# Three weight loads of 2 MB moved on SyncE's DMA queue, between two layers of a one-core kernel

## What is computed

```python
p = h @ w_in                                   # 1024 -> 3 x 1024
p = sum(pp[:, j:j + L] * conv_w[j] for j in range(3)) + conv_b
x0, x1, v = split(p, 3)
h_fwd, h_bwd = hyena_filter(L, w1, b1, w2, b2, w3, freq)
z = v * x1
z = bidir_long_conv(z, h_fwd, h_bwd) + bias * z
y = (x0 * z) @ w_out
```

## Time and profile before

| | |
|---|---|
| Time, median of 3 runs | 1439.36 us (1438.39 to 1439.51) |
| The profiled execution's own time | 1443.63 us, span 1441.70 us |
| Mean granted TensorE clock | 0.968 |
| TensorE busy | 1300.4 us (90%) |
| VectorE busy | 641.2 us (44%) |
| ScalarE busy | 300.6 us (21%) |
| HBM read | 496.57 MB, 348 GB/s over the span |

### The profile page before, as it was taken

The page is one execution under the profiler, slowest core; times in us unless marked ns, Lnnn a source line. Parts: engine busy times, 40 slices in busy tenths (PEclk is TensorE's granted clock), DMA queues, the critical chain, the costliest instruction groups (busy, mean ns, idle before and its releaser), DMA issues.

```text
span 1441.7 us, 21888 instructions
## 1 busy us (share of the span) xinstructions
PE 1300.4 (90%) x9044; PEld 676.9 (47%) x9044; DVE 641.2 (44%) x1175; ACT 300.6 (21%) x508; POOL 60.2 (4%) x112
## 2 busy tenths in 40 slices
PE   4999888899999979889898999999999978988898
PEld 1445335764444424333345776874454433333344
DVE  5998862254333322222333678854433322232232
ACT  2226341321111111111112113131111111111111
POOL 0010581000000000000000000000000000000000
PEclk9999999999999999999998999989999999999999
DMA  9663874959999999999999872587999999999996
GB/s 380 226 212 87 162 221 183 394 233 376 417 421 421 426 427 427 429 423 430 426 418 341 316 275 117 217 351 298 372 425 422 422 428 426 425 430 428 428 420 271
DMA packets 54327, 502.78 MB, mean 349 GB/s; under 512 B 9740, under 2 KB 16652, under 8 KB 20236
## 3 DMA queue, kind: packets, MB, share of 16 engines
q1 hardware_dynamic: 53676, 499.18, 86.3%
q10 hardware_dynamic: 544, 2.10, 0.4%
HBM read 496.57 MB, written 4.69 MB: 348 GB/s over the span
## 4 chain that ended last, share of the span: by engine, by line
PE 61%; DMA 28%; DVE 7%; issue 2%; SPq 1%; ACT 1%; DVEq 0%; ACTq 0%
PE ps L753 56%; DMA arena<-in_w_experts 23%; DMA arena<-in_ada_w 4%; PE ps L1071 2%; PE ps L446 2%; SPq L490 1%; DVE arena L2052 1%; ACT arena L1419 1%; DVE arena L1879 0%; DMA arena<-in_mcst 0%; DVE arena L2245 0%; PE ps L806 0%; DVE arena L1874 0%; DVE arena L1875 0%; DVE arena L1892 0%
## 5 line engine op out<-in xcount | busy, mean ns | idle before, releaser
L753 PE MATMUL ps<-arena 128*32 128x512 f32 (+10 forms) x8224 | 1216.1, 485 | 122.2 <-issue 44.9
L753 PEld LDWEIGHTS ps<-arena 128*32 128x32 f32 (+5 forms) x8224 | 614.7, 130 | 708.4 <-issue 582.2
L1419 ACT ACTIVATE arena<-ps 128x512 f32<-128x512 f32 (+6 forms) x305 | 168.5, 552 | 923.3 <-PE ps L753 767.5
L1419 ACT ACTIVATE arena<-arena 128x256 f32<-128x256 f32 (+7 forms) x143 | 94.6, 683 | 152.6 <-DVE arena L2113 58.3
L2093 DVE SCALAR_TENSOR_TENSOR arena<-arena,ps 128x256 f32<-128x256 f32 x44 | 21.2, 481 | 228.4 <-ACT arena L1419 228.4
L2111 DVE CAST arena<-ps 128x512 bf16<-128x512 f32 x42 | 29.1, 692 | 165.5 <-PE ps L753 165.5
L2048 DVE COPY arena<-ps 128x512 f32<-128x512 f32 x44 | 30.4, 692 | 128.4 <-PE ps L753 128.4
L2081 DVE TENSOR_TENSOR arena<-arena 128x1024 bf16<-128x1024 f32 x42 | 51.5, 1226 | 37.3 <-ACT arena L1419 37.0
L1071 PE MATMUL ps<-arena 128*128 128x128 f32 x352 | 52.8, 273 | 0.0
L2113 DVE TENSOR_TENSOR arena<-ps,arena 128x1024 f32<-128x1024 f32 x42 | 51.4, 1225 | 1.4
L743 POOL MEMSET arena<- 128x1 f32 x2 | 0.2, 102 | 1186.2 <-PE ps L1071 1186.2
(11 more groups left out here) (234 smaller groups left out, 483.6 us busy)
## 6 DMA issues: line engine op xcount, KB each, us to landing
arena<-in_w_experts SPq DMA_DIRECT2D x70, 3072.0 KB, 20.6
arena<-in_w_experts SPq DMA_DIRECT2D x98, 1024.0 KB, 13.6
arena<-in_w_experts SPq DMA_DIRECT2D x38, 2048.0 KB, 19.7
arena<-in_ada_w SPq DMA_DIRECT2D x40, 1024.0 KB, 6.7
arena<-in_hy_w_in SPq DMA_DIRECT2D x6, 2048.0 KB, 13.7
arena<-in_ada_w SPq DMA_DIRECT2D x4, 2048.0 KB, 23.0
arena<-in_w_shared SPq DMA_DIRECT2D x2, 3072.0 KB, 10.1
arena<-in_hy_w_out SPq DMA_DIRECT2D x1, 4096.0 KB, 12.1
```

Of the source, the lines that this page charges most:

```text
L753: return pe.matmul(out, lhsT, rhs, start=start, stop=stop, skip_group_check=skip)
L1419: return act.activation(out, in_, func, **kw)
```

## The change

The loads of the first three parts of the Hyena input matrix leave `moe_loads(0)`, where they stood between the waits for `dn_mm` (NG - 1) and `dn_mm` (DOWNS). Part 0 is now issued behind `moe_loads(0)`, which ends with the check for crowded experts, and ahead of the wait for `moe_x`; part 1 behind `f_w2` and ahead of block 16; part 2 behind the last of `fw_in` and ahead of block 17. Nothing else is changed.

```diff
                 if li == 0:
                     sp.wait_ge(sem("hscr_out"), 16)
                     sp.wait_ge(sem("dn_mm"), NG - 1)
-                    for n in range(3):
-                        load(hyw[:, n], A["hy_w_in"][HYP[n]], f"hyw_in{n}")
                 sp.wait_ge(sem("dn_mm"), (li + 1) * DOWNS)
                 sp.wait_ge(sem("hscr_out"), 16 * (li + 1))
...
             first_experts(0, (2,))
             moe_loads(0)
 
+            load(hyw[:, 0], A["hy_w_in"][HYP[0]], "hyw_in0")
             sp.wait_ge(sem("moe_x"), KD)
...
             load(at(HC["zemb"], L), A["hcst"][:, HCST["zemb"][0]:HCST["zemb"][0] + L], "fw_in")
             load(f_w1, A["f_w1"], "fw_in")
             load(f_w2, A["f_w2"], "fw_in")
+            load(hyw[:, 1], A["hy_w_in"][HYP[1]], "hyw_in1")
             ada_load(LATER)
             load(f_w3, A["f_w3"], "fw_in")
             for name in ("ic", "is"):
                 load(at(HC[name], L), A["hcst"][:, HCST[name][0]:HCST[name][0] + L], "fw_in")
             for name, width in (("decay", HYW), ("fc", P), ("fs", P)):
                 load_by_parity(HC[name], name, width)
+            load(hyw[:, 2], A["hy_w_in"][HYP[2]], "hyw_in2")
             for n in range(3, 6):
                 ada_load(LATER + 2 * n - 5)
```

## The result

| | before | changed | ratio, 95% interval |
|---|---|---|---|
| median of 6 runs | 1437.93 us | 1451.44 us | 1.0091 [1.0076, 1.0106] |
| the changed kernel once more, beside 23 runs of before | 1439.61 us | 1448.41 us | 1.0062 [1.0043, 1.0080] |
| profiled execution, span | 1441.7 us | 1447.9 us | |

Slower, by 13.5 us in the first comparison and 8.8 us in the second. The two profiled executions differ by 6.2 us only, and that has a reason which all later readings must respect: the stretch ahead of the change, the same instructions in both kernels, ended 4.0 us sooner in the changed kernel's profile.

A forecast was written before the change was run, and what follows sets the result against it. Between the layers the bound was taken to be block 17's second half, landing behind a DMA backlog. Its delay of 6.9 us plus 1.8 us of low clock gave 1439.4 + 8.7 = 1448.1 us; range 1445.5 to 1450.5, 8 in 10 1442.5 to 1452.0.

The forecast's parts named there:

- the two terms of the sum: Between MoE layer 0 and project(1): block 17 landing later, +6.9 us, and TensorE's lowered clock behind that wait, +1.8 us.
- Step 1: SyncE's dn_mm waits lose their loads: SyncE gains nothing and the expert loads are not sped up.
- Step 2: SyncE's exit from the crowded-expert branch: taken as 0.5 us, hyw 0 issued at 769.5 and landing at 776.4, ahead of project(0).
- Rival C: SyncE leaves the check's branch as slowly as TensorE, delaying hyw 0 and everything behind it: 1453.4 us, chance 0.10.
- Step 3: Crowded-expert check of layer 0: gets cheaper without hyw loads on the DMA engines, 3.4 us taken, between zero and 3.8.
- Step 4: SyncE's queue behind the check: hyw 1 issued at 775.0, block 17 landing at 808.2 against 801.3, +6.9 us.
- Step 5: Block 17's second half is asked for at 789.9, before the queue runs dry, full until 808: no cost.
- Step 6: TensorE's wait for block 17 lowers its clock: 3.5 us at half rate behind it, +1.8 us, bounds 0 and 2.6.
- Step 7: From 802.38 to the filtered spectrum TensorE sets the chain, with no wait group above 1.0 us up to 946: the shift stays.
- The sum: Whole kernel: 6.9 us for block 17 plus 1.8 us for the clock, 8.7 us slower, 1448.1 us.
- Rival A: Cheaper check is kept and block 17 isn't late, as hyw loads fill the small-packet stretch: -3.4 us, 1436.0 us, chance 0.11.
- Rival B: Most idle queue time is filled in the small-packet stretch: block 17 at 803.8, +2.5, no clock drop, 1441.9 us, chance 0.09.

The follow-up runs named there:

- e2: Changed kernel with all three hyw loads issued together behind the check, ahead of the wait for moe_x: 1450.9 us, ratio 1.0071.
- e1: Changed kernel with hyw 2 issued behind both halves of block 17 instead of ahead of them: 1447.2 us, ratio 1.0042.
- e11: e7 with the ada_w block for VectorE (block 18 first) asked for ahead of the hyw part in three later rounds: 1434.6 us, ratio 0.9966.
- e6: Changed kernel with hyw 0 at its old place, hyw 1 behind the check ahead of the moe_x wait, hyw 2 behind block 17: 1440.5 us, ratio 0.9998.
- e5: Changed kernel with 18 idle TensorE products added ahead of block 17's products, in the wait for that block: 1448.6 us, ratio 1.0063.
- e7: e6 with block 17's products moved on TensorE from behind project(0) to behind the first quarter of project(1): 1438.1 us, ratio 0.9992.
- e10: Changed kernel with 22 idle TensorE products added ahead of block 17's products, in the wait for that block: 1451.7 us, ratio 1.0090.

## Why the prediction was right

The direction and the mechanism held, and both times lie within the 1442.5 to 1452.0 us given for 8 in 10. The first, 1451.4 us, is above the forecast's own range of 1445.5 to 1450.5, and that the second, 1448.4, comes so near to the forecast of 1448.1 is luck in part: counted from W, the two terms of the sum came to 12.5 us where 8.7 had been summed, and 1 to 2 us came back later that no step had foreseen. Point by point:

- **Step 1**, no effect on the experts: held as far as it shows. TensorE's last two waits for expert weights were 0.90 and 0.87 us, against 1.14 and 0.88.
- **Step 2**, SyncE leaves the branch fast: held. hyw 0 was issued at 765.68, about 0.5 us behind the branch, W + 5.1 in place of the W + 4.9 foreseen. Rival C is out. The time to land was under-sized: 8.8 us, not 6.9.
- **Step 3**, the check gets cheaper: held. The eight additions ended at W + 9.3 (766.74 + 3.22) in place of W + 12.1, 2.8 us won for 3.4 foreseen, and the branch took 3.49 us. In the eleven profiles in which hyw 0 alone or nothing was in the queue when the branch began it took 3.33 to 3.95, in the three with all three loads 5.93 to 6.34. In e2 all three were asked for 0.5 us behind the branch, and it took 3.70. What the prediction did not see is where the gain ends: the first addition needs products of TensorE that were done 5.7 us behind W, and in the changed kernel it is they that released it. The Trainium skill (Runtime: NRT & Kernel Launch, Instruction fetch mechanics) has a taken branch wait for a DMA fetch; the traces agree. The packets of instructions in them moved 1 to 2 us behind TensorE's branch in the changed kernel (766.2 to 767.2) and 2 to 4 us behind it before (771.2 to 773.2), so the fetch came later while data was being moved.
- **Step 4**, block 17 late by 6.9 us: right in kind, too small. hyw 1 went out at W + 11.2, not W + 10.4, and from there block 17 took 34.3 us, not 33.2; it came 8.8 us late. The sum of work in the queue (36.1 us) carried the forecast to within 2 us.
- **Step 5**, nothing runs dry: held, though block 16 landed at W + 26.9 and not W + 22.2. The chain goes through it only because the issue of block 17's second half comes behind it; by then the queue still had 15 us of work.
- **Step 6**, the clock: the term that was mis-sized most. I took 1.8 us with a bound of 2.6, from a recovery of 3.5 us; it measured 3.7, with recovery 8 us behind the start of the dense work. The row I read it from followed a stretch with some work in it, not a full stop; whether that makes the difference no run tests. And ahead of `project(0)` the clock did not fall at all in the changed kernel (granted clock 1.00 up to 792, 64 records in 14.09 us in place of 15.81), where I had let it fall in both. Those 1.7 us went into the wait for block 17 and changed nothing.
- **Step 7**, the shift stays: held to within 1 to 2 us of 12.5; what gives these back stays open.
- **The sum**, 8.7 us: the ledger has 12.5 us at block 19, 10.2 to 11.8 at the end; the timed runs say 13.5 and 8.8. The ends of the forecast's own range are about half a microsecond wider than the terms named for them give (1439.4 + 6.5 = 1445.9 and 1439.4 + 7.9 + 2.6 = 1449.9).

Rival A needed block 17 by 798, W + 33.4, and it came at W + 45.5; taking one 2 MB load from ahead of it brought it 4.7 us sooner (e1), about that load's 4.9 us. The order is not a strict one, though: from W to W + 45.6 the queue moved 13.79 MB where 12.74 were asked for up to block 17, so about 1 MB of hyw 3, issued behind it, had moved before its last part landed. A gain from the cheaper check can be had, but only where block 17 doesn't hold it up (e11). Rival B needed block 17 at W + 39.2; the stretch of small packets was as slow as before (200 to 218 GB/s in 784 to 790, against 179 and 255).

## What to carry to other kernels

A queue that works in order makes one transfer's lateness another one's. Before a load is moved, ask which transfer is waited for last behind it, and whether the engines would have been idle in the time it leaves; here 6 MB asked for later left the engines idle for 6 us, and a transfer that the diff doesn't name came 8.8 us late. In this kernel a gain ahead of such a wait was worth nothing until the waited-for transfer, and then the next one of its kind, were moved up as well.

## What the runs showed that I had not expected

- The stretch up to W, all but the same in every kernel, took between 757.84 and 764.97 us in the profiles, and W was at 760.63 and 764.65 in two profiles of the very same kernel. That is more than most effects here; without a mark to count from, the first two profiles would have shown little more than half of the loss.
- The clock went down behind a wait of 6.43 us (e6), and behind two pauses of 1.45 and 1.35 us with eight light products between them (e5), and behind 0.99 and 2.17 us with eight between them (e7), but not behind the single 1.35 us of the kernel before, nor in e10 without a pause.
- Each full-sized load takes 4.9 us in a full queue and 8.8 us from issue to landing in an empty one: the gap between is more than the 2.0 us that a small store suggested.
- The taken branch of this check costs TensorE 3.3 to 4.0 us with free DMA engines and 5.9 to 6.3 with busy ones. VectorE's costs 5.8 with busy ones (767.7 to 773.51) and at most 3.0 with free ones (763.7 to 766.74, where it was TensorE's product that it waited for). SyncE and ScalarE, with short bodies, take half a microsecond.
